# LN1 passes of the later token tiles moved into the first FFN groups, and the last FFN tile computed in two column quarters

## The reference

```
mix = jnp.einsum('bsd,de->bse', g_a * y_a + g_b * y_b, w_o[l])
x = _layernorm(ALPHA * x + mix, ln1_g[l], ln1_b[l])
hid = jnp.square(jax.nn.relu(jnp.einsum('bsd,df->bsf', x, w_ff1[l])))
ffn = jnp.einsum('bsf,fd->bsd', hid, w_ff2[l])
x = _layernorm(ALPHA * x + ffn, ln2_g[l], ln2_b[l])
```

## Time and profile before

| | us |
|---|---|
| median of 3 runs | 1176.18 (1176.17 to 1176.6) |
| the profiled execution | 1173.57 |
| its span, slowest core (core 0) | 1172.0 |
| spans of the 8 cores | 1167.1 to 1172.0 |
| PE busy on core 0 | 1131.5 |
| DVE busy | 520.5 |
| ACT busy | 274.7 |

### The profile page before, as it was taken

One profiled execution on the slowest core, in us unless ns is written; L12 is line 12 of the kernel. 1 busy time (PEld: TensorE's weight loads), 2 busy tenths in 40 slices (PEclk: granted clock), 3 DMA queues, 4 the chain that ended last, 5 costly groups with the idle time before them and its releaser, 6 DMA issues.

```text
span 1172.0 us, 15316 instructions; the slowest of 8 cores (1167.1 to 1172.0 us)
## 1 busy us (share of the span) xinstructions
PE 1131.5 (97%) x5483; PEld 522.2 (45%) x5594; DVE 520.5 (44%) x741; ACT 274.7 (23%) x416; POOL 137.2 (12%) x252
## 2 busy tenths in 40 slices
PE   6899999999999999999998999999999999999996
PEld 2454444444444444444443444444444444444442
DVE  0545465322248433502188545642222853342347
ACT  0224422211125333100011443221111353330000
POOL 3002200000011010100120121000000101000012
PEclk8999999999999999999999999999999999999998
DMA  9975785455552384664448438554434307544402
GB/s 134 178 130 104 142 135 118 61 81 81 90 91 38 65 133 72 109 118 80 72 86 179 95 94 171 104 82 76 61 66 78 63 0 115 87 84 76 72 37 108
DMA packets 29594, 110.36 MB, mean 94 GB/s; under 512 B 3536, under 2 KB 3536, under 8 KB 29008
## 3 DMA queue, kind: packets, MB, share of 16 engines
q0 software_dynamic: 23616, 88.36, 47.4%
q1 hardware_dynamic: 5904, 21.02, 5.6%
HBM read 189.33 MB, written 8.39 MB: 169 GB/s over the span
## 4 chain that ended last, share of the span: by engine, by line
PE 88%; issue 4%; DMA 4%; DVE 3%; ACT 1%; POOL 0%; DVEq 0%; ACTq 0%; POOLq 0%
PE ps L260 87%; DMA ring<-wblk 4%; DVE regQ L725 1%; ACT regP L729 1%; DVE regQ L802 0%; DVE regP L486 0%; PE ps L263 0%; DVE t L481 0%; POOL ring L143 0%; POOL regR L143 0%; DVE st L727 0%; ACT t L480 0%; DVE regQ L804 0%; DVE st L734 0%; DVEq L129 0%
## 5 line engine op out<-in xcount | busy, mean ns | idle before, releaser
L260 PE MATMUL ps<-regR,ring 128*128 128x512 bf16 x2880 | 658.4, 380 | 19.3 <-DMA ring<-wblk 10.1
L260 PEld LDWEIGHTS ps<-regR,ring 128*128 128x128 bf16 x2944 | 285.5, 98 | 357.4 <-issue 25.4
L260 PE MATMUL ps<-ring,regP 128*128 128x512 bf16 x1003 | 220.2, 379 | 1.1
L143 POOL DMA_DIRECT2D ring<-wblk x150 | 80.5, 541 | 777.8 <-PE ps L260 775.3
L260 PEld LDWEIGHTS ps<-ring,regP 128*128 128x128 bf16 x1024 | 100.2, 98 | 120.8
L260 PE MATMUL ps<-regP,ring 128*128 128x512 bf16 x626 | 147.2, 379 | 0.7
L774 DVE TENSOR_TENSOR regP<-t 128x512 bf16<-128x512 f32 x128 | 88.0, 692 | 124.8 <-ACT t L773 124.8
L773 ACT ACTIVATE t<-ps 128x512 f32<-128x512 f32 x128 | 75.9, 597 | 134.6 <-PE ps L260 129.0
L260 PEld LDWEIGHTS ps<-regP,ring 128*128 128x128 bf16 x640 | 62.6, 98 | 75.5 <-issue 0.5
L812 DVE SCALAR_TENSOR_TENSOR regQ<-regQ,ps 128x512 f32<-128x512 f32 x32 | 22.0, 688 | 132.8 <-PE ps L260 132.6
L480 ACT ACTIVATE t<-ps 128x512 f32<-128x512 f32 x48 | 28.6, 598 | 195.8 <-PE ps L260 159.0
(11 more groups left out here) (60 smaller groups left out, 584.5 us busy)
## 6 DMA issues: line engine op xcount, KB each, us to landing
ring<-wblk POOLq DMA_DIRECT2D x130, 512.0 KB, 7.5
bigW<-wbig POOLq DMA_DIRECT2D x4, 2048.0 KB, 22.8
regQ<-x SPq DMA_DIRECT2D x16, 512.0 KB, 4.9
y<-regQ SPq DMA_DIRECT2D x16, 512.0 KB, 3.2
ring<-wblk POOLq DMA_DIRECT2D x16, 384.0 KB, 10.0
regR<-xT POOLq DMA_DIRECT2D x8, 512.0 KB, 14.2
ring<-wblk POOLq DMA_DIRECT2D x4, 256.0 KB, 14.6
t<-ln1g SPq DMA_DIRECT2D x2, 512.0 KB, 9.6
```

Source lines behind the costliest of these rows:

```text
L143: self.items.append(lambda e, out=out, in_=in_, sem=sem: e.dma_start(out=out, in_=in_).then_inc(sem, 16))
L260: return lambda e: e.matmul(out, lhsT=l, rhs=r, start=st, stop=sp_)
```

## The change

In stage O, `step` gives way to two lists. `early[k]` says what is called in step k beside `head(k)`: transposes (`tail`) ahead of the head, the bf16 copy (`xbf`, the former call of `affine`) and `mid` behind it. `late` holds what is called between the first 16 groups of F1, now behind groups 2, 5, 8, 11 and 14. The negated mean (line 727) is made on ACT. In stage F2 of the last supertile's second half, tile 7 leaves the first loop; at the end it is computed in two passes over all 32 chunks, each 256 columns wide, the second into bank 0, with a drain for each. `ln2_final` of a tile is called right after that tile's own drain, and for tile 7 in two column halves with two stores.

```
-                OP(dve, lambda e: e.tensor_scalar(out=s1[:, 1:2], in0=s1[:, 0:1], scalar1=-1.0 / D, scalar2=None, op0=ALU.mult),
+                OP(act, lambda e: e.activation(out=s1[:, 1:2], in_=s1[:, 0:1], func=AF.Copy, scale=-1.0 / D),
...
+            def xbf(tt):
+                affine(tt, xbt[tt % 3], xbB[tt % 3], b1)
+
+            early = [[], [(mid, 0)], [(xbf, 0), (mid, 1)], [(tail, 0), (xbf, 1), (mid, 2)], [(tail, 1), (xbf, 2), (mid, 3)], [(tail, 2), (xbf, 3)], [(tail, 3)], [(mid, 4)]]
+            late = [[(xbf, 4), (mid, 5)], [(tail, 4), (xbf, 5), (mid, 6)], [(tail, 5), (xbf, 6), (mid, 7)], [(tail, 6), (xbf, 7)], [(tail, 7)]]
             for k in range(8):
-                step(k)
+                before = [x for x in early[k] if x[0] is tail]
+                for f, tt in before:
+                    f(tt)
+                head(k)
+                for f, tt in early[k]:
+                    if f is not tail:
+                        f(tt)
...
-                    if n % 3 == 0 and drain:
+                    if n % 3 == 2 and drain:
                         drain.pop(0)()
...
+            for p in range(parts):
+                cs_ = slice(p * n, (p + 1) * n)
+                OP(dve, lambda e, cs_=cs_: e.scalar_tensor_tensor(out=rq[tt][:, cs_], in0=rq[tt][:, cs_], scalar=s2[:, 18:19], in1=g2rep[:, cs_], op0=ALU.subtract, op1=ALU.mult),
+                   reads=[rqB[tt], st2B[tt], g2B], writes=[rqB[tt]])
...
                 for q in range(8 - lb):
-                    for tt in range(8):
+                    for tt in range(7 if split else 8):
                         f2_part(st, h, tt, [q])
...
                 for tt in range(8):
+                    if split and tt == 7:
+                        for quarter in range(2):
+                            f2_part(st, h, tt, list(range(8)), quarter)
+                            f2_drain(tt, h, quarter)
+                        ln2_final(st, tt, 2)
+                        break
                     f2_part(st, h, tt, list(range(8 - lb, 8)))
                     f2_drain(tt, h)
-                    if last and h == 1 and tt:
-                        ln2_final(st, tt - 1)
+                    if split:
+                        ln2_final(st, tt)
```

More of the change, by code:

```diff
@@ L190, in build_program @@
         st1t = [sb(f"st1_{i}", [128, 8], F32) for i in range(8)]
-        st2t = [sb(f"st2_{i}", [128, 16], F32) for i in range(8)]
+        st2t = [sb(f"st2_{i}", [128, 24], F32) for i in range(8)]
         ps = es.enter_context(nc.psum_tensor("ps", [128, 8, 512], F32))
@@ L746, in tail, with run @@
                 OP(act, lambda e: e.activation(out=x1Tb[:, :, ts_], in_=psb[:, b0, :, :], func=AF.Copy), reads=[bankB[b0]], writes=[x1bB[tt]])
[L748 to L756, removed]
-            for k in range(8):
-                step(k)
+            def xbf(tt):
+                affine(tt, xbt[tt % 3], xbB[tt % 3], b1)
+            early = [[], [(mid, 0)], [(xbf, 0), (mid, 1)], [(tail, 0), (xbf, 1), (mid, 2)], [(tail, 1), (xbf, 2), (mid, 3)], [(tail, 2), (xbf, 3)], [(tail, 3)], [(mid, 4)]]
+            late = [[(xbf, 4), (mid, 5)], [(tail, 4), (xbf, 5), (mid, 6)], [(tail, 5), (xbf, 6), (mid, 7)], [(tail, 6), (xbf, 7)], [(tail, 7)]]
+            for k in range(8):
+                before = [x for x in early[k] if x[0] is tail]
[5 more added lines that the diff above has]
+                        f(tt)
             if st + 1 < ST:
                 load_big(0)
-            return [lambda k=k: step(k) for k in range(8, 11)]
+            def run(ops):
+                for f, tt in ops:
+                    f(tt)
+            return [lambda ops=ops: run(ops) for ops in late]
         def f1_group(st, fc, half):
@@ L798, in build_program, with ln2_final @@
         pending_tails = []
-        def ln2_final(st, tt):
+        def ln2_final(st, tt, parts=1):
             s2 = st2t[tt]
[L802 to L805, removed]
@@ L820, in f2_part @@
-        def f2_part(st, h, tt, qs):
+            n = 1024 // parts
+            for p in range(parts):
+                cs_ = slice(p * n, (p + 1) * n)
+                OP(dve, lambda e, cs_=cs_: e.scalar_tensor_tensor(out=rq[tt][:, cs_], in0=rq[tt][:, cs_], scalar=s2[:, 18:19], in1=g2rep[:, cs_], op0=ALU.subtract, op1=ALU.mult),
+                   reads=[rqB[tt], st2B[tt], g2B], writes=[rqB[tt]])
+            for p in range(parts):
+                cs_ = slice(p * n, (p + 1) * n)
+                B = rqB[tt] if parts == 1 else Buf()
+                OP(dve, lambda e, cs_=cs_: e.scalar_tensor_tensor(out=rq[tt][:, cs_], in0=rq[tt][:, cs_], scalar=s2[:, 21:22], in1=b2rep[:, cs_], op0=ALU.mult, op1=ALU.add),
+                   reads=[rqB[tt], st2B[tt], b2B], writes=[B])
+                out_toks.append(DMA(sp, y_d[r0:r0 + 128, cs_], rq[tt][:, cs_], rq_st[tt] if p == 0 else rq_st[(tt + p) % 8], reads=[B]))
@@ new lines, in f2_drain @@
+        def f2_drain(tt, h, quarter=None):
+            s2 = st2t[tt]
+            c0 = h * 512 + (quarter or 0) * 256
+            n = 512 if quarter is None else 256
+            o = h * 6 + (quarter or 0) * 6
+            cs_ = slice(c0, c0 + n)
+            bank = tt if not quarter else 0
+            OP(dve, lambda e: e.scalar_tensor_tensor(out=rq[tt][:, cs_], in0=rq[tt][:, cs_], scalar=ALPHA, in1=ps[:, bank, 0:n], op0=ALU.mult, op1=ALU.add),
+               reads=[bankB[bank], rqB[tt]], writes=[rqB[tt]])
+            OP(dve, lambda e: e.bn_stats(out=s2[:, o:o + 6], in_=rq[tt][:, cs_]), reads=[rqB[tt]], writes=[st2B[tt]])
+            if h == 1 and quarter != 0:
+                oe = o + 6
+                OP(dve, lambda e: e.bn_aggr(out=s2[:, 18:20], in_=s2[:, 0:oe]), reads=[st2B[tt]], writes=[st2B[tt]])
+                OP(dve, lambda e: e.tensor_scalar(out=s2[:, 20:21], in0=s2[:, 19:20], scalar1=LN_EPS, scalar2=None, op0=ALU.add), reads=[st2B[tt]], writes=[st2B[tt]])
+                OP(pool, lambda e: e.tensor_tensor(out=s2[:, 21:22], in0=s2[:, 20:21], in1=chalf[:, 0:1], op=ALU.pow), reads=[st2B[tt], memB], writes=[st2B[tt]])
@@ L821, in f2_part @@
+        def f2_part(st, h, tt, qs, quarter=None):
             ts_ = slice(tt * 128, (tt + 1) * 128)
+            bank = tt if not quarter else 0
+            cs_ = slice(0, 512) if quarter is None else slice(quarter * 256, quarter * 256 + 256)
+            n = cs_.stop - cs_.start
             fns = []
@@ L830, in f2_part @@
                     hb.append(hidB[fc][tt // 4])
[L831 to L832 removed]
+                    fns.append(mm(ps[:, bank, 0:n], hid[:, fc, ts_], W[:, k, cs_], fc == 0, fc == 31))
+            PEG(fns, reads=wb + hb, writes=[bankB[bank]])
         def stage_F2(st, b1):
@@ L855, in stage_F2 @@
             cur[0] = 0
-            if last:
-                ln2_final(st, 7)
-            else:
+            if not last:
                 for tt in range(8):
```

16 lines of the change are left out of this document (5 added, 11 removed).

## The result

The changed kernel is slower: ratio to the kernel before 1.019, 95% interval 1.0172 to 1.0208, which is +22.4 us on 1176.2, so about 1198.6. The forecast was 1208 with a range of 1194 to 1222; its mechanism is what the trace shows, and one term, the clock, was far too large. The profiled execution took 1198.68 us around a span of 1197.0 (core 5), against 1173.57 and 1172.0: +25.0 in the span.

A forecast was written before the change was run, and what follows sets the result against it. The prediction took TensorE, busy 97% of the span, as the bound. Stage O's loops +18.1, clock +13.6 and end +0.6 made +32.3 us, so 1208 us from a median of 1176.18, range 1194 to 1222.

The forecast's parts named there:

- the clock: Stage O: TensorE's clock falls once at each of eight gaps, 1.7 us each, +13.6 us in all.
- The closed loop: Stage O: head, drain, copy, transposes wait in turn, period 7.00 us, TensorE standing 3.11; +18.1 us with the FFN's extra transposes.
- third case: Stage O: every gap trips the clock and it stays at half rate between gaps; 1226 us, chance 0.20.
- The end: Last supertile's end: line 812 waits for POOL's power, VectorE falls behind, quarter matmuls hide behind its backlog; +0.6 us.
- 2 to 3 us would be gained if the last quarter were drained at once: Sign of a wrong forecast, at the end: last quarter drained as soon as computed, the end gaining 2 to 3 us.
- Line 727, costed at 0: Stage O: moving it to ScalarE costs 0.1 to 0.2 us either way, covered by the 3 us gaps.
- the forecast's own range: Whole kernel: 1201 to 1216 us, with the clock costing 6 to 21 us; chance 0.58.
- rival 1: Stage O: the clock holds through the gaps, leaving 18.1 + 0.6; 1195 us, chance 0.14.
- Rival 3: Stage O: the copy's order does not bind, as VectorE has slack; waits go, the end gains 2.9; 1168 us, chance 0.05.
- Rival 2: Stage O: the clock falls and stays low, heads between gaps run at 1.2 GHz; 1226 us, chance 0.20.
- Rival 4: Stage O: the queue was misread, both stages cost nothing and only the end shows; 1177 us, chance 0.03.

The follow-up runs named there:

- e2: The changed kernel with the bf16 copy called ahead of the head again, transposes unmoved: 1176.65 us, ratio 1.0016 to the kernel before.
- e3: The changed kernel with 12 unread 512-wide matmuls ahead of each early set of transposes, to fill TensorE's gaps: 1195.17 us, ratio 1.017 to the kernel before.
- e7: The kernel before with only the end's part of the change, plus an own buffer record for the second LayerNorm's power: 1173.74 us, ratio 0.9994.
- e8: The kernel before with only line 727, the negated mean, moved to ScalarE: 1173.21 us, ratio 0.9986.
- e1: The changed kernel with the transposes of tiles 0 to 3 one head later: 1168.77 us, ratio 0.995 to the kernel before.

## Why the prediction was right, and where it was off

- The closed loop. Right in place, number and cause: four gaps per stage, each ended by line 710, on all cores. The period is 6.93 instead of 7.00, because the copy starts 1.14 us after the drain's start, not 1.33 (I had kept the time at which line 727 had started); the gap is 2.75 to 2.9 instead of 3.11. The bubbles come to 16.2 + 0.9 = 17.1 against the 18.1 predicted. e2 shows the cause: the copy's place alone gives 20 of the 22 us back.
- The clock. The mis-sized term, 13.6 predicted. The price of one fall was right (1.7 from the earlier trace rows; 1.5 to 1.7 measured). The number was not: I took "one fall of 1.7 for each gap", and 27 of 64 gaps had one, five of eight on the slowest core of the profiled execution, 7.8 us; by the runs (e3) the term is 5.1, with about 3 either way. I had set one core with a fall against one without, and the trace of before has more: the gap of 2.67 to 2.68 us near 32 us stands on all eight cores, and the clock fell on six of them and held on cores 2 and 6. Here is core 2's window behind it, as in the earlier trace rows:

```profile
33.00:36.50 3.50, 3.50 (x38) 1.86 (x36) 0.56 (x2) 1.70 (x4) 0.02 (x1) 1.00 1.05 178
```

  Six of eight would give 10.2 us for eight gaps, still too much. The Trainium skill ("TensorE: Matmul & The Clock Gate", "Why this matters for your kernels") warns against idle gaps a little longer than these, as ones behind which TensorE is back at half rate. In this trace fewer than half of the gaps of 2.75 to 2.9 us come with a fall. The prediction takes this rule for its third case, in which the clock stays low, though one fall at every gap is what its own sum has; neither came.
- The end. Predicted +0.6, measured −0.1. The wait for POOL's power came as worked out (0.95 us), but the period is 5.44 and not 5.64: the drain that follows line 817 starts 1.21 us after it, where I had 1.39, the distance of two passes of which the second reads the first's output. So the backlog is 1.6 us and not 2.8. The 256-wide products took half of the 512-wide ones, as assumed (0.109 us), and did hide behind it. The stretch behind VectorE's last pass, taken as unchanged, grew by 0.3 us. That 2 to 3 us would be gained if the last quarter were drained at once came true for VectorE's end only: in e7 the end is 1.5 us shorter than before in the trace, and its time is 0.7 less with an interval that takes in no change.
- Line 727, costed at 0. Alone on the kernel before it gains 1.6 us (e8). In the changed kernel it doesn't lie inside the gaps as I wrote: drain and copy are both on the loop, and line 727 stood between them. From drain to copy are now 1.14 us, where 1.51 were in the earlier trace rows, and the 1.33 of the prediction had taken off half of that. What it is worth in the changed kernel is not shown, since no run has that kernel with line 727 on VectorE.
- The sum. 17.1 + 7.8 − 0.1 = 24.8 on the profiled execution, whose span grew by 25.0; by the ratio of the runs, 22.4. The first lies at the lower edge of the forecast's own range, +25 to +40 (1201 to 1216), the second under it, and both inside the full range of 1194 to 1222, which was made wide enough for rival 1. In size the result is nearer to rival 1 (1195) than to the forecast (1208): the loops are right to a microsecond, and of the clock neither case came, since it fell at some gaps and held at most.
- The rivals. Rival 3 (faster, VectorE has slack) was half right: VectorE has the slack, as e1 shows, but not the order. Rival 2 is refuted, since the clock always came back after 3.4 us. Rival 4 is refuted by the stages' 41.3 us.

Not settled: why one gap of 2.75 us costs the clock and the same gap on another core doesn't. The rows of cores 2 and 5 show no difference in what TensorE did before their first gap, and the gaps at which the clock falls differ from core to core and from the first stage to the second.
